# Layer 0's experts with earlier row fetches, paired chunk steps and nine held chunks; layer 1's scan with keys and queries multiplied in place

## What is computed

```
aff = softmax(einsum('bnd,de->bne', h, w_router))
gate, idx = top_k(swapaxes(aff, 1, 2), 2 * N // 16)
xe = h[bidx, idx]
hid = silu(einsum('becd,edf->becf', xe, w_gate)) * einsum('becd,edf->becf', xe, w_up)
ye = einsum('becf,efd->becd', hid, w_down) * gate[..., None]
return zeros_like(h).at[bidx, idx].add(ye)
```

```
q = silu(p[1]);  k = (1 - lb) * sigmoid(-z);  f = lb + (1 - lb) * sigmoid(z)     # exp(logf)
A[t, s] = sum_d q[t, d] * k[s, d] * prod(f[s+1..t, d])       # s <= t in a chunk
o = (q * decay from the chunk's start) @ S + A @ v           # only latent rows are needed
S = decay of the whole chunk * S + (k * decay to the chunk's end).T @ v
```

## Time and profile before

| | us |
|---|---|
| median of 3 runs (2777.17 to 2781.77) | 2777.96 |
| profiled execution | 2788.23 |
| its span in the trace | 2786.4 |
| layer 0's experts, from the end of its routing to the rows' way back | 890 to 1517 |
| layer 1's projections of the scan, then `hgrn_silu` | 1782 to 1962, to 1966 |
| layer 1's scan | 1966 to 2139 |
| layer 1's experts | 2268 to 2750 |
| PE busy over the span | 2325.1 (83%) |
| DVE busy over the span | 941.0 (34%) |
| POOL busy over the span | 303.1 (11%) |

### The profile page before, as it was taken

The page is one execution under the profiler, slowest core; times in us unless marked ns, Lnnn a source line. Parts: engine busy times, 40 slices in busy tenths (PEclk is TensorE's granted clock), DMA queues, the critical chain, the costliest instruction groups (busy, mean ns, idle before and its releaser), DMA issues.

```text
span 2786.4 us, 39245 instructions
## 1 busy us (share of the span) xinstructions
PE 2325.1 (83%) x16421; PEld 1216.8 (44%) x16421; DVE 941.0 (34%) x2142; ACT 460.8 (17%) x994; POOL 303.1 (11%) x320
## 2 busy tenths in 40 slices
PE   4789999688894999999997796899356959988896
PEld 2446556577682222222222474558344712222221
DVE  0134334577534111222121207400687332221123
ACT  1224112312301000000000105300533100000000
POOL 0000000233102311101011200000142030000000
PEclk9889999778896999999999899999667979999997
DMA  7100452000402899999999212011002459999995
GB/s 260 54 31 1 174 213 106 17 3 3 159 32 87 326 357 332 350 355 363 341 346 354 75 46 77 16 61 50 27 2 94 149 223 409 409 410 410 410 410 211
DMA packets 165690, 539.90 MB, mean 194 GB/s; under 512 B 14576, under 2 KB 49840, under 8 KB 159152
## 3 DMA queue, kind: packets, MB, share of 16 engines
q1 hardware_dynamic: 149920, 492.99, 46.2%
q0 software_dynamic: 7008, 24.12, 3.0%
q10 hardware_dynamic: 8624, 20.80, 2.1%
HBM read 519.53 MB, written 18.35 MB: 193 GB/s over the span
## 4 chain that ended last, share of the span: by engine, by line
PE 37%; DMA 8%; DVE 8%; issue 7%; SPq 6%; ACT 2%; POOLq 1%; POOL 0%; ACTq 0%; DVEq 0%
PE bank L2614 7%; PE bank L458 7%; SPq L2455 6%; DMA arena<-in_moe_w_up_dram 4%; PE bank L488 4%; PE bank L2569 3%; PE bank L2554 3%; PE bank L2575 2%; PE bank L2623 2%; PE bank L2194 2%; DMA arena<-tok_ctx_dram,arena 2%; PE bank L2541 2%; DVE arena L2003 1%; DVE small L779 1%; PE bank L2526 1%
## 5 line engine op out<-in xcount | busy, mean ns | idle before, releaser
L458 PE MATMUL bank<-arena,ring 128*128 128x384 f32 (+1 forms) x704 | 247.3, 514 | 11.3 <-DVEq L2979 8.5
L2554 PE MATMUL bank<-ring,arena 128*64 128x512 f32 x896 | 218.7, 609 | 6.0 <-DMA ring<-in_moe_w_gate_dram 4.8
L2569 PE MATMUL bank<-ring,arena 128*64 128x512 f32 x896 | 212.4, 595 | 13.0 <-DMA ring<-in_moe_w_up_dram 13.0
L458 PEld LDWEIGHTS bank<-arena,ring 128*128 128x128 f32 x704 | 135.6, 193 | 122.0 <-issue 35.2
L2799 DVE TENSOR_TENSOR arena<-arena,bank 128x512 f32<-128x512 f32 x32 | 21.9, 686 | 438.8 <-PE bank L2580 315.0
L449 DVE COPY arena<-bank 128x384 f32<-128x384 f32 (+2 forms) x50 | 26.7, 534 | 360.0 <-PE bank L458 234.0
L2194 PE MATMUL bank<-ring,arena 128*128 128x256 f32 x640 | 143.3, 387 | 1.1 <-DVEq L2979 1.1
L2614 PE MATMUL bank<-ring,arena 128*64 128x512 f32 x512 | 136.3, 636 | 0.7 <-ACT arena L2701 0.7
L2691 ACT ACTIVATE arena<-bank 128x512 f32<-128x512 f32 x32 | 19.1, 597 | 710.2 <-PE bank L2554 710.2
L2614 PE MATMUL bank<-arena 128*64 128x512 f32 x512 | 127.6, 608 | 7.1 <-ACT arena L2698 6.5
L2194 PEld LDWEIGHTS bank<-ring,arena 128*128 128x128 f32 x640 | 124.0, 195 | 19.1 <-DVEq L2979 1.7
(11 more groups left out here) (382 smaller groups left out, 3262.4 us busy)
## 6 DMA issues: line engine op xcount, KB each, us to landing
ring<-in_moe_w_gate_dram SPq DMA_DIRECT2D x112, 1024.0 KB, 9.0
ring<-in_moe_w_up_dram SPq DMA_DIRECT2D x112, 1024.0 KB, 10.8
ring<-in_moe_w_down_dram SPq DMA_DIRECT2D x64, 1024.0 KB, 9.1
arena<-in_moe_w_down_dram SPq DMA_DIRECT2D x64, 1024.0 KB, 18.4
ring<-in_w_mod_dram SPq DMA_DIRECT2D x48, 1024.0 KB, 7.0
ring<-in_odd_w_in_dram SPq DMA_DIRECT2D x16, 1024.0 KB, 5.4
arena<-in_moe_w_gate_dram SPq DMA_DIRECT2D x16, 1024.0 KB, 18.8
arena<-in_moe_w_up_dram SPq DMA_DIRECT2D x16, 1024.0 KB, 19.7
```

The costliest lines, as they stand in the source:

```text
L458: mm = nc.tensor.matmul(bk[:, 0:b_ - a], lhs(k), rhs(k, a, b_), start=k == 0, stop=k == kb - 1)
L2554: mm = nc.tensor.matmul(G_[half(hf), :], xl[:, k, :], columns(g, kk, hf), start=k == 0, stop=k == KB - 1)
L2569: mm = nc.tensor.matmul(U_[half(hf), :], xl[:, k, :], columns(u, kk, hf), start=k == 0, stop=k == KB - 1)
```

## The change

It has two parts, one in layer 0's experts and one in layer 1's scan. Layer 1's experts and all other stages keep their work.

**Layer 0's experts.** POOL's `fetch` moves between the two `add_rows` of a pair and is for two pairs on. PE's steps take two chunks of each kind at a time: `gate_up_both` runs the latent matmuls of two gate and two up chunks, then the context ones of all four; `down_both` the latent ones of two down chunks, with four `gather` blocks between them, then the context ones. SP holds nine chunks in place of six: three more buffers lie in the arena (`SPARE_AT`), first filled when routing's logits are done (`rt["logc"]`), and signalled by `sum_back`. PE's loop over pairs is written out.

```
+ def stream_in_order(sp):                      # held = RING + 3
+     if q >= held:  sp.wait_ge(*chunk_done(*order[q - held]))
+     elif q >= RING: sp.wait_ge(rt["logc"], 1)
...
- def scatter_rows(i, first_pair=False):
-     for e in range(2): add_rows(i, e, first_pair)
+     add_rows(i, 0, first_pair)
+     if fetches: fetch(i + 2)
+     add_rows(i, 1, first_pair)
...
- with nc.gpsimd.Fori(1, NP - 1) as i:
-     gates(i); fetch(i + 1); scatter_rows(i)
+ with nc.gpsimd.Fori(1, NP - 2) as i:
+     gates(i); scatter_rows(i, False, True)
...
+ def gate_up_both(i, e):
+     for jj in (0, 2):
+         for j in (jj, jj + 1):  # latent columns: gate chunk j, then up chunk j
...
+         for j in (jj, jj + 1):  # context columns of both chunks
```

```
+ project("hgrn_projections", jobs, act_after={n_q + 2: queries_ready, n_q + n_z + 2: first_gates})
- phase("hgrn_silu", act=act)
...
+ def grown(x, n, d, j, side, other):
+     v = split(x, j)[:, :, :, side, :]
+     by = siblings(n, d, j, other)               # broadcast over the block
+     return nc.vector.tensor_tensor(v, v, by, ALU.mult)
...
+ for l in range(1, NL):                          # DVE, a latent tile
+     for d in range(2):
+         nc.vector.wait_ge(hg["att_used"], at_level(n, l, d))
+         grown(QB[n % 2][d], n, d, l - 1, QSIDE[d], KSIDE[d])
+         grown(KS[n % 2][d], n, d, l - 1, KSIDE[d], QSIDE[d])
+     if l < NSM: merge(n, l, 0); merge(n, l, 1)
+     if l in (2, 3): states(n - 1, l - 2)
...
+ for n in range(NT):                             # ACT
+     if 1 < n + 1 < NT: hgrn_gates(n + 1)        # waits hg["turn"] of tile n - 1
+     turned_keys(n - 1, 0); turned_keys(n - 1, 1)
+     ... AT copies of tile n
```

More of the change, by code:

```diff
@@ L1773, in hgrn_scan @@
         def hgrn_scan():
-            at = iter(list(range(0, 6144, 512)) + list(range(10240, 14336, 512)))
-            S = bufs(next(at), next(at))
-            R_, QC, KC, KF, QF, AT, KRT = (bufs(next(at), next(at)) for _ in range(7))
-            KS = [bufs(next(at), next(at)) for _ in range(2)]
+            S, AT, KRT = (hg_pair() for _ in range(3))
+            QB = [hg_pair() for _ in range(2)]
+            FB = [hg_pair() for _ in range(2)]
+            KS, tile, decays = HKS, hg_tile, hg_decays
@@ L1932, in act @@
+            def act():
+                nc.scalar.activation(SG, SG, ACT.Silu)
+                for n in range(NT):
+                    if 1 < n + 1 < NT:
+                        hgrn_gates(n + 1)
+                    for d in range(2):
+                        if n and not is_lat(n):
+                            turned_keys(n - 1, d)
                     if is_lat(n):
                         for d in range(2):
+                            turned_keys(n - 1, d)
+                        for d in range(2):
@@ new lines, in dve @@
+                    if not is_lat(n):
+                        for j in range(LEVELS):
+                            dv.settle()
+                            for d in range(2):
+                                ins = grown(KS[n % 2][d], n, d, j, KSIDE[d], QSIDE[d])
+                                if j < LEVELS - 1:
+                                    dv(ins)
+                                else:
+                                    ins.then_inc(hg["fin"], 1)
+                                next_products(n, d, j)
+                        if n:
+                            for d in range(2):
+                                states(n - 1, d)
+                        continue
@@ L2062, in hgrn_scan @@
+                for d in range(2):
+                    states(NT - 1, d)
             phase("hgrn_scan", pe=pe, act=act, dve=dve, pool=pool)
@@ L2662, in pe @@
                     gather(0, k)
-                pair(0, True, False)
-                with nc.tensor.Fori(1, NP - 1) as i:
-                    pair(i, False, False)
-                pair(NP - 1, False, True)
+                if skewed:
+                    for i in range(NP):
+                        skewed_pair(i, i == 0, i == NP - 1)
+                else:
+                    pair(0, True, False)
+                    with nc.tensor.Fori(1, NP - 1) as i:
+                        pair(i, False, False)
+                    pair(NP - 1, False, True)
                 if not with_ctx:
```

561 lines of the change are left out of this document (295 added, 266 removed).

## The result

The changed kernel takes 2714.53 us (median of 4 runs, 2708.94 to 2715.25), where the kernel before took 2779.86 beside it: a ratio of 0.976, 95% interval 0.974 to 0.978. Run again on another chip beside other kernels it took 2707.43 (2711 to 2718 was expected of that run) against 2777.45, a ratio of 0.975 (0.974 to 0.977). So the change is worth 65 to 70 us. The forecast was 64, to 2714.

What follows compares the result with a forecast made beforehand. PE sets layer 0's experts, DVE the scan, DMA layer 1's unchanged experts. Savings of 28 us (fetch 17, double steps 11) and 36 in the scan make 64: median 2714 us, range 2690 to 2743.

Steps and rivals of the forecast that it cites:

- The scan: Layer 1, last projection copy to last state update: 176 us becomes 140, saving 36, range 20 to 50.
- The walk: Tile-by-tile sum of the scan with its chain through ACT: first latent tile at 24.5 us, 138 in all.
- growths at 0.34: DVE in the scan: 140 new in-place multiplications at 0.34 us each, 47.6 us together.
- The cover for gates 0 and 1: Gates of scan tiles 0 and 1 hide in the projections, where PE is the pace; otherwise some 16 us show.
- POOL's port: Scan: POOL's eight queries block DVE on the shared port for about 2 us, up to 14 by the skill's rule.
- Layer 0's fetch: Layer 0's experts: fetching rows earlier removes PE's wait before the first gather, 2.85 us in six pairs, 17 us.
- Layer 0's double steps: Layer 0's experts: half the switches between 64 and 32 columns go, saving 11 us, bounds 0 and 12.
- Nine chunks at nothing: Layer 0's experts: three more chunk buffers cost or gain nothing, since SP waits for slots and not the reverse.
- (a): Layer 0: DMA or slots already set the pace, PE waits for weights, a pair stays near 76 us; 2740, chance 0.13.
- (b): Scan: gates and turned keys run under DVE's own work, so the scan is 128 us; time 2700, chance 0.14.
- (c): Scan: in-place growth is slow, all 224 new DVE operations at 0.94 us; time 2833, chance 0.06.
- (d): Layer 0 and scan: both parts move waits and save no time; 2778, chance 0.02.

Runs made afterwards that it cites:

- the scan alone: The kernel before with only the change's layer 1 scan put in, layer 0's experts left as they were: 2739.56 us.
- the state updates later: On the kernel with the ring rotated, DVE's state updates behind levels 3 and 4, not 2 and 3, and ACT's small A blocks copied first: 2682.72 us.
- the fetch alone: The kernel before with only the row fetch moved between the two experts' `add_rows` and made for two pairs on: 2765.07 us, ratio 0.995.
- six chunks: The changed kernel with the ring's six chunks in place of nine, double steps and early fetch kept: 2759.62 us, ratio 0.994.
- turned keys first: The changed kernel with ACT's turned keys of the tile ahead put in front of the next gates in the scan: 2688.99 us, ratio 0.966.
- gathers one place later: On the kernel with turned keys first, each layer 0 gather block one place later among the down matmuls: 2681.99 us.
- the ring rotated: On the kernel with gathers one place later, layer 1's first weight chunk takes the ring slot layer 0 frees first: 2678.29 us, ratio 0.965.

## Why the prediction was right, point by point

**The total.** 64 us forecast, 65 and 70 measured, 2714 against 2714.53. It is right by its steps in the scan. In layer 0 the mechanisms were right and the sizes were not: the stage fell by 31.5 to 34.9 us where 28 stood, with the fetch taken 1 to 5 us too high and the double steps and nine chunks 8 too low; 3 us were then given back behind the stage, which the prediction did not have. So errors of both signs lie under the sum, and that it came within 1 us is luck, as the second timing, 2707.43, shows.

**The scan**: 36 forecast, 38 by the traces (mean of six 135.4 against 173.4 in three), 40 by the run alone. The walk held tile by tile, to 1.3 us. Its terms: growths at 0.34 from start to start (2.85 us for 14 products is 0.20 each, the value taken, and not the 3.3 that the prediction set beside it; the group's busy means, 420 and 242 ns, are longer since one starts before the last has ended); 3.94 us to DVE's start, taken as 4; waits of 9.30 and 8.72, taken as 9.5, of 5.36 in tile 2, taken as 4, and of 2.68 in tile 5, taken as 3.6. The clock, which moves this stage by 5 us from one execution to the next, is in no term. The cover for gates 0 and 1 held: DVE's copies in the projections stand 6.9 us apart with the gates between ACT's, as before. And the chain is what the walk said it is, since 7.8 us of gates taken out of it took 6.7 and 7.4 off the waits of tiles 3 and 4 (6.0 and 7.1 against the scan alone, at nearly the same clock).

**POOL's port.** A product of 16 elements that began while POOL made its first query took 1.24 us where its like took 0.17. The timeline of POOL and of DVE in after:

```profile
1948.93 1.54 POOL L2008 TENSOR_TENSOR arena<-arena 128x512 f32<-128x512 f32 x1 [12.59 <-ACT arena L1815]
```

```profile
1949.27 1.24 DVE L2013 TENSOR_TENSOR arena<-arena 128x16 f32<-128x16 f32 x1
...
1950.76 0.17 DVE L2013 TENSOR_TENSOR arena<-arena 128x16 f32<-128x16 f32 x1
```

The Trainium skill, "SBUF — State Buffer", section "SBUF: two separate sides", has the loser of the shared port pair blocked for the whole instruction. The trace agrees: the product ended as the query did, at 1950.5. That it cost 1.1 us, where 2 were taken, and not up to 14 is a matter of place: six of the eight queries ran while DVE waited or worked from a bank, and one, begun while a growth ran, took 1.81 us itself in place of 1.26 to 1.28. With the state updates later the place is another, and two more queries cost 0.8 us each. The 0.94 and 0.34 that the prediction set side by side are a length and a distance of starts; the length alone was 0.41.

**Layer 0's fetch**: 17 forecast, 12 (time) and 12.5 to 15.9 (stage) measured. The mechanism and the count of six were right; 2.85 a pair was too much, at 2.1 to 2.65, and about half of what the trace of before lost is the clock behind the stall, not the stall (PE busy 553.0 us in the stage, 544.4 with the fetch alone). The 0.85 left for DVE was right: 0.8 to 0.9.

**Layer 0's double steps**: 11 forecast, 15.2 in the stage (9 to 16 in time). Here the step that failed is the price of a switch. I took eight latent matmuls at 1.76 us from a run that follows a switch and so holds part of its cost. In after four such runs stand in a row:

```profile
1007.90 1.94 PE L2637 MATMUL bank<-ring,arena 128*64 128x512 f32 x8
1009.67 1.89 PE L2646 MATMUL bank<-arena 128*64 128x512 f32 x8
1011.39 1.89 PE L2637 MATMUL bank<-arena 128*64 128x512 f32 x8
1013.10 1.89 PE L2646 MATMUL bank<-arena 128*64 128x512 f32 x8
```

The inner ones start 1.72 apart, and from a gate chunk to an up chunk there nothing is lost. With that, a gate step's three runs are 5.16 and its switches 0.27, a down step's one and a half 2.58 and 0.29: a double gate step saves 0.27 and a double down step 0.29, two of each 1.12 per half, and 1.16 was measured. That the width is what costs, and not something else that changes with it, is read from these starts and not tested apart. My bound of 12 was too low for the same reason.

**Nine chunks at nothing**: as a gain, 3.8 us missed (with the loop written out), since PE did wait for weights in the first pair. As a cover it was the largest of all: 47 us of layer 0 hang on it (581.2 against 534.4). The prediction named what it covers (four chunks held, five places free) and gave no price for its loss.

**What the prediction did not have**: the 3 to 5 us given back behind layer 0, where the first chunks of layer 1 meet the rows' way back. The list of what moves named POOL's queue and SP's waits within the stage, but not that the slot in which a stage's last chunk lies sets when the next stage's first load starts.

**The rivals.** (a) fell: pairs at 71.6 and SP waiting 439 us for PE. With six chunks it would have been right, at 78.3 us a pair. (b), the chain holding less, fell in after and is what the kernel with turned keys first made true: 115 us. (c) fell: 0.42 mean for the growths. (d) fell: both stages are shorter.

The fastest version found here has turned keys first, gathers one place later and the ring rotated: 2678.29 us, 0.965 of before, some 29 us below the change.

## What to carry to other kernels

When work is put on another engine's list, look at what else in that list now stands between a result and the one who waits for it: an early preparation for the next tile costs its full length if it stands ahead of a copy that the present tile needs, and little behind it (1.8 us here). A buffer count that looks idle because the loader waits for slots can still be the condition for a change that releases slots in bunches; and at a stage's end the slot in which the last chunks lie decides when the next stage's loads start, and what they collide with. The same move can place another engine's work beside yours on a shared port, as the later state updates did. To price a switch between two kinds of work, take the pure rate from the middle of a long run, not from the run behind a switch.

## What the runs showed of the hardware

A stall of 2.5 us in an otherwise unbroken row of matmuls was followed by the lower clock, and the same work behind it took 10.72 us at 0.53 granted in place of 6.27 at 1.00; the clock fell so behind five of six stalls of 2.0 to 3.2 us in one kernel and behind four of six of 1.8 to 2.9 in another, and their length doesn't tell which. A change of matmul width between 64 and 32 columns and back costs PE 0.27 to 0.29 us here, read from halves of 34.19 us and 33.03 that differ in the order of the same matmuls alone. The way back of the rows (indirect adds, then reads) took 13.0 to 13.1 us of DVE's waiting where the weight loads had started ahead of layer 0's last turn by 3 us or more, and 16.0 to 17.7 with six 1 MB loads running through it. A multiplication of DVE with both inputs in SBUF that began while one of POOL ran ended with it (1.24 us in place of 0.17); DVE's state updates, which read a bank, took their usual 0.69 and 1.12 us beside POOL. And the scan of one and the same code, in six executions, was between 132.2 and 137.9 us long, at granted clocks of 0.78 down to 0.69, so a gain of 3 us in such a stage needs several traces, and the clock of each, beside it.
